# Gathers of half rows onto 128 partitions, with four 128x128 turns per tile, in a mixture-of-experts stage

## What is computed

```python
def hierarchical_moe(h, ...):          # h: 512 rows of 1024
    g_sel = argmax(softmax(h @ w_rg + b_rg))            # 1 of 4 groups
    e_logits = (h @ w_re + b_re)[group g_sel]           # 8 experts of it
    top_p, top_i = top_k(softmax(e_logits), 2)
    weights = top_p / sum(top_p) * p_gsel
    # for each row t and each of its 2 experts e, weight w:
    #   out[t] += w * (silu(h[t] @ w_gate[e]) * (h[t] @ w_up[e])) @ w_down[e]
```

## Time and profile before

| | us |
|---|---|
| Three runs, median (lowest to highest) | 1374.76 (1373.16 to 1378.31) |
| Profiled execution, its own time | 1375.67 |
| Its span, first to last instruction | 1374.0 |
| PE busy | 1277.7 (93%) |
| DVE busy | 611.6 (45%) |
| ACT busy | 351.0 (26%) |
| POOL busy | 158.7 (12%) |
| Mean granted TensorE clock | 0.976 of full speed |
| Read from HBM, written | 299.49 MB, 13.75 MB |

### The profile page before, as it was taken

The page is one execution under the profiler, slowest core; times in us unless marked ns, Lnnn a source line. Parts: engine busy times, 40 slices in busy tenths (PEclk is TensorE's granted clock), DMA queues, the critical chain, the costliest instruction groups (busy, mean ns, idle before and its releaser), DMA issues.

```text
span 1374.0 us, 20748 instructions
## 1 busy us (share of the span) xinstructions
PE 1277.7 (93%) x7392; PEld 637.2 (46%) x7393; DVE 611.6 (45%) x1058; ACT 351.0 (26%) x759; POOL 158.7 (12%) x278
## 2 busy tenths in 40 slices
PE   5999999999999999999999999989989987897887
PEld 1446656678844444644455545433333333332322
DVE  1667787874223343268787525212212212122225
ACT  1323233321144442212478310111101101010112
POOL 4011111111010000000000002311121121121110
PEclk9999999999999999999999999999999999899999
DMA  9163624331191110042131565879999999999995
GB/s 373 66 261 78 231 73 169 140 108 43 36 293 47 46 31 0 0 159 77 52 142 50 199 264 208 306 313 394 407 416 420 401 401 421 404 408 405 403 389 214
DMA packets 40570, 304.00 MB, mean 221 GB/s; under 512 B 7980, under 2 KB 8132, under 8 KB 22944
## 3 DMA queue, kind: packets, MB, share of 16 engines
q1 hardware_dynamic: 31952, 285.12, 52.9%
q0 software_dynamic: 8528, 17.67, 4.2%
HBM read 299.49 MB, written 13.75 MB: 228 GB/s over the span
## 4 chain that ended last, share of the span: by engine, by line
PE 72%; DMA 12%; DVE 9%; ACT 3%; issue 2%; POOL 1%; DVEq 0%; ACTq 0%; SPq 0%; POOLq 0%
PE bank L886 19%; PE bank L2994 13%; DMA arena<-in_w_down 9%; PE bank L3012 8%; PE bank L817 8%; PE bank L932 3%; PE bank L994 2%; PE bank L2979 2%; DMA arena<-in_ada_w 2%; DVE side L1524 1%; PE bank L1008 1%; PE bank L1238 1%; PE bank L1182 1%; PE bank L1159 1%; DVE X L3271 1%
## 5 line engine op out<-in xcount | busy, mean ns | idle before, releaser
L886 PE MATMUL bank<-hT,arena 128*128 128x512 f32 x656 | 290.0, 597 | 0.0
L2994 PE MATMUL bank<-arena,hT 128*64 128x512 f32 x1012 | 229.1, 603 | 16.6 <-DMA arena<-in_w_gu 15.2
L886 PEld LDWEIGHTS bank<-hT,arena 128*128 128x128 f32 x656 | 122.8, 191 | 147.0 <-issue 143.5
L2994 PEld LDWEIGHTS bank<-arena,hT 128*64 128x64 f32 x1012 | 71.8, 138 | 153.7 <-issue 134.6
L3012 PE MATMUL bank<-arena,yT 128*64 128x512 f32 x512 | 125.5, 635 | 12.7 <-DMA arena<-in_w_down 10.9
L3182 DVE TENSOR_SCALAR hT<-hT 128x256 f32<-128x256 f32 x32 | 9.4, 294 | 246.7 <-ACT hT L3120 246.7
L817 PE MATMUL bank<-arena,yT 128*128 128x512 f32 x256 | 114.8, 603 | 2.4 <-DVE yT L1785 2.3
L3120 ACT ACTIVATE hT<-bank 128x256 f32<-128x256 f32 x32 | 12.3, 383 | 263.2 <-PE bank L2994 263.2
L817 PEld LDWEIGHTS bank<-arena,yT 128*128 128x128 f32 x256 | 48.2, 192 | 60.3 <-issue 56.5
L3012 PEld LDWEIGHTS bank<-arena,yT 128*64 128x64 f32 x512 | 36.5, 145 | 76.9 <-issue 62.4
L932 PEld LDWEIGHTS bank<-arena 64*64 64x64 f32 x1856 | 59.4, 135 | 23.5 <-issue 13.1
(11 more groups left out here) (498 smaller groups left out, 1697.3 us busy)
## 6 DMA issues: line engine op xcount, KB each, us to landing
arena<-in_w_gu SPq DMA_DIRECT2D x62, 2048.0 KB, 24.5
arena<-in_w_down SPq DMA_DIRECT2D x32, 2048.0 KB, 30.6
arena<-in_w_in SPq DMA_DIRECT2D x53, 512.0 KB, 3.6
arena<-in_ada_w SPq DMA_DIRECT2D x24, 1024.0 KB, 5.2
arena<-in_w_ada SPq DMA_DIRECT2D x8, 1024.0 KB, 9.4
arena<-in_w_out SPq DMA_DIRECT2D x8, 1024.0 KB, 9.3
arena<-in_w_ada SPq DMA_DIRECT2D x8, 512.0 KB, 7.4
arena<-expert_rows SPq DMA_DIRECT2D x4, 1024.0 KB, 8.4
```

The source lines that it names most:

```text
L886: last = T.matmul(bank[0:rows, :], w[:, k, 0:rows], hT[:, k, :], start=k == 0, stop=k == KD - 1)
L2994: last = T.matmul(banks[1 + ub][MT * h:MT * h + MT, :], tile.xT[:, k, :], weights[:, :, 256 * h:256 * h + 256], start=k == 0, stop=k == KD ...
```

## The change

The rows are stored with permuted columns: column m*8 + k of a row goes to place k*128 + m. The DRAM scratch is seen as 1024 half rows of 2 KB. The numbers in `slots` are those of half rows, on all 128 partitions: positions 0 to 63 of a tile's first halves, then of its second halves. For that PE makes the slots' product twice, and DVE adds a column (`half_row`, -4 and -3) in the last of its three instructions. A gather brings 128 half rows onto 128 partitions x 512. Four transposes of 128 x 128 over contiguous columns take the place of eight of 64 x 128, and DVE's two instructions of `rows_in` read and write in another order. Two clears and the place of a one-row helper change with the buffers.

```diff
@@ -782,7 +782,11 @@
             V.wait_ge(s_sq_rows, NORM0 + TT * (i - 1) + t + 1)
             if i == 2 and t >= 2:
                 V.wait_ge(s_xnst, 16 * (t - 1))
-            dve.done(V.tensor_scalar(xn_tiles[i - 1][t], X[:, t, :], rstd[:, t:t + 1], None, MUL))
+            if i == 2:
+                dve.done(V.tensor_scalar(xn_tiles[1][t].rearrange("p (k m) -> p m k", k=KD),
+                                         X[:, t, :].rearrange("p (m k) -> p m k", k=KD), rstd[:, t:t + 1], None, MUL))
+            else:
+                dve.done(V.tensor_scalar(xn_tiles[i - 1][t], X[:, t, :], rstd[:, t:t + 1], None, MUL))
             V.sem_inc(s_xn, 1)
 
         def dve_hT_tile(i, t):
@@ -2311,7 +2315,8 @@
             pe_busy(bank, 7)
             eng.wait_ge(s_hot, 1)
             for n in range(2 * TT):
-                last = T.matmul(bank[0:MT, 0:NE + NOV], hot_pos[:, n, :], hot_tile[:, n, :], start=n == 0, stop=n == 2 * TT - 1)
+                for q in range(2):
+                    last = T.matmul(bank[MT * q:MT * q + MT, 0:NE + NOV], hot_pos[:, n, :], hot_tile[:, n, :], start=n == 0, stop=n == 2 * TT - 1)
             full(last)
             bank = fill(("places",))
             pe_busy(bank, 1)
@@ -2585,13 +2590,14 @@
         r_ones = ones[:, 0:NE]
         places = iotas[:, 0:NE + NOV]
         wts = sb("wts", [P, 2, TT])
-        slots = sb("slots", [MT, NE + NOV + 2], u32)
+        slots = sb("slots", [P, NE + NOV + 2], u32)
         ov_first = sb("ov_first", [1, 2 * NE - 2], i32)
         KEPT_AT = NE + 1
         last_hot = hT[:, 4, 0:TT * MT].rearrange("p (t m) -> p t m", m=MT)
         s_rt_in, s_rt_exp, s_routed = sem("router_ready_for_exp"), sem("router_exp_made"), sem("routed")
         s_xnst = sem("xn_stored")
         xn_dram = nc.dram_tensor("xn_scratch", [SEQ, DM], fp32, kind="Internal").ap()
+        xn_half = xn_dram.rearrange("t (h n) -> (t h) n", h=2)
 
         def bc(a, n):
             return a.rearrange("p (t o) -> p t o", o=1).to_broadcast([P, TT, n])
@@ -2676,10 +2682,9 @@
             dve.done(V.scalar_tensor_tensor(r_kept, r_nov[0:1, 0:NE - 3], 0.0, r_incl[0:1, 0:NE - 3], ALU.is_gt, MUL))
             V.tensor_copy(ov_first[:, KEPT_AT:KEPT_AT + NE - 3], r_kept)
             bank = take(V, ("slots",))
-            v = r_v[0:MT]
-            done(V.tensor_scalar(v, bank[0:MT, 0:NE + NOV], 0.0, 1024.0, ALU.is_equal, MUL))
-            empty(V, "dve", V.scalar_tensor_tensor(v, bank[0:MT, 0:NE + NOV], -1.0, v, ADD, ADD), ("slots",))
-            done(V.tensor_copy(slots[:, 0:NE + NOV], v))
+            done(V.tensor_scalar(r_v, bank[:, 0:NE + NOV], 0.0, 4.0 * SEQ, ALU.is_equal, MUL))
+            empty(V, "dve", V.scalar_tensor_tensor(r_v, bank[:, 0:NE + NOV], 2.0, r_v, MUL, ADD), ("slots",))
+            done(V.tensor_scalar(slots[:, 0:NE + NOV], r_v, half_row, 2.0, ADD, ADD))
             eng.sem_inc(s_routed, 1)
             second = hot_pos[:, TT:KT, :]
             done(V.tensor_scalar(r_half, second, 0.0, 0.5, ALU.is_gt, MUL))
@@ -2732,10 +2737,10 @@
 
         first, more_ = Steps("first"), Steps("extra")
 
-        tiles = [Tile(u, yflat[0:MT, 1024 * u:1024 * u + 1024], hflat[:, 512 * u:512 * u + 512],
+        tiles = [Tile(u, yflat[:, 512 * u:512 * u + 512], hflat[:, 512 * u:512 * u + 512],
                       hflat[:, 1536 + 256 * u:1792 + 256 * u], yflat[:, 3072 + 256 * u:3328 + 256 * u],
                       hflat[:, 2304 + 512 * u:2816 + 512 * u]) for u in range(U)]
-        extra = Tile("extra", side[0:MT, 0:1024], side[:, 1024:1536], side[:, 1536:1792], side[:, 1792:2048],
+        extra = Tile("extra", side[:, 0:512], side[:, 1024:1536], side[:, 1536:1792], side[:, 1792:2048],
                      cactB[:, :, :].rearrange("p k m -> p (k m)"))
         w_gu = [[sem(f"gate_up_loaded_{u}_{half}") for half in range(2)] for u in range(U)]
         w_dn = [sem(f"down_loaded_{u}") for u in range(U)]
@@ -2751,7 +2756,7 @@
         s_placed_col = [sem("first_places_picked"), sem("extra_places_picked")]
         s_extra_kept = sem("extra_rows_kept")
         place_col = sb("place_col", [P, U + 2], u32)
-        idx_col = sb("idx_col", [MT, U + 1], u32)
+        idx_col = sb("idx_col", [P, U + 1], u32)
 
         def stand_alone(eng):
 
@@ -2884,7 +2889,7 @@
             done = pool.done
             done(G.memset(ones_row, 1.0))
             eng.dma_start(gain_row, A["final_g"].rearrange("(o n) -> o n", o=1)).then_inc(s_gateB, 16)
-            done(G.memset(yflat[0:MT, 0:3072], 0.0))
+            done(G.memset(yflat[:, 0:512 * U], 0.0))
             done(G.memset(slots[:, NE + NOV:NE + NOV + 2], 4 * SEQ))
             eng.wait_ge(s_routed, 1)
 
@@ -2892,8 +2897,8 @@
                 G.tensor_copy(idx_col[:, i:i + 1], slots[:, bass.ds(e, 1)]).then_inc(picked, 1)
                 eng.wait_ge(picked, n + 1)
                 stand_alone(eng)
-                eng.indirect_dma_start(tile.xg, None, xn_dram, bass.IndirectOffsetOnAxis(ap=idx_col[:, i:i + 1], axis=0),
-                                       bounds_check=SEQ - 1, oob_is_err=False).then_inc(tile.gathered, 16)
+                eng.indirect_dma_start(tile.xg, None, xn_half, bass.IndirectOffsetOnAxis(ap=idx_col[:, i:i + 1], axis=0),
+                                       bounds_check=2 * SEQ - 1, oob_is_err=False).then_inc(tile.gathered, 16)
 
             def scatter(tile, steps, i, e, picked, n):
                 eng.wait_ge(steps.rows, n + 1)
@@ -2953,7 +2958,7 @@
             experts(eng, body)
 
         s_spread, s_copied = sem("last_places_then_gain_spread"), sem("last_places_then_gain_copied")
-        gain_row, ones_row = yflat[64:65, 0:DM], yflat[64:65, DM:DM + P]
+        gain_row, ones_row = yflat[64:65, 512 * U:512 * U + DM], yflat[64:65, 512 * U + DM:512 * U + DM + P]
 
         yg = slot_w[2][:, 0:8192].rearrange("p (n d) -> p n d", d=DM)
         finalG = slot_w[2][:, 8192:9216]
@@ -2975,8 +2980,8 @@
                     eng.wait_ge(steps.xT, n + 1)
                 eng.wait_ge(tile.gathered, (turn + 1) * 16)
                 stand_alone(eng)
-                for k in range(KD):
-                    last = T.transpose(banks[bank][:, MT * k:MT * k + MT], tile.xg[:, k::KD], ident[0:MT, 0:MT])
+                for j in range(KD // 2):
+                    last = T.transpose(banks[bank][:, CH(j)], tile.xg[:, CH(j)], ident[:, :])
                 last.then_inc(tile.xf, 1)
 
             def gate_up(tile, steps, u, e, n, ub, it=None, last_quarter=False):
@@ -3164,7 +3169,7 @@
             hidden_out(tiles[LAST[1]], first, NE - 1)
 
         def dve_experts(eng):
-            A2, B2 = (a.rearrange("p (k o) -> p k o", o=1).to_broadcast([P, KD, MT]) for a in (AB[2], modc[4]))
+            A2, B2 = (a.rearrange("p (q j o) -> p q j o", q=2, o=1).to_broadcast([P, 2, KD // 2, MT]) for a in (AB[2], modc[4]))
 
             for steps in (first, more_):
                 eng.sem_inc(steps.xT, 1)
@@ -3172,9 +3177,10 @@
             def rows_in(tile, steps, n, turn, bank=0):
 
                 eng.wait_ge(tile.xf, turn + 2)
-                V.tensor_tensor(tile.xT, b3(banks[bank][:, :], MT), A2, MUL).then_inc(steps.xT_own, 1)
+                xT = tile.xT.rearrange("p (q j) m -> p q j m", q=2)
+                V.tensor_tensor(xT, banks[bank][:, :].rearrange("p (j q m) -> p q j m", q=2, m=MT), A2, MUL).then_inc(steps.xT_own, 1)
                 eng.wait_ge(steps.xT_own, n + 1)
-                V.tensor_tensor(tile.xT, tile.xT, B2, ADD).then_inc(steps.xT, 1)
+                V.tensor_tensor(xT, xT, B2, ADD).then_inc(steps.xT, 1)
 
             def clamped(tile, steps, n):
 
```

## The result

The kernel after takes 1355.28 us (median of 6 runs, 1353.61 to 1357.33) against 1373.96 (median of 6) for the one before: a ratio of 0.9868, with a 95% interval of 0.985 to 0.9887. The medians lie 18.7 us apart, and by the ratio the kernel is 1.3% faster. The forecast was 1374.3, and the range of 1367 to 1380 doesn't hold the result. One of the runs of before took 1479.11 us: it was disturbed and is not in the ratio, but it is among the six of the median, which is 1373.16 without it (17.9 us).

The account below looks back on a forecast made before the run. The weights' DMA stream was taken to bound the experts' stage, so only PE's chain before 918 us counts: turns -1.9, slots' product +1.2, DVE +0.2, sum -0.5 us, forecast 1374.3, range 1367 to 1380.

Parts of the forecast that it names:

- a fixed amount of transfers: Behind SP's weight load issued at 918.04: the end is that issue plus these transfers plus a tail.
- Gathers on 128 partitions: Fetching the experts' rows: same bytes, order stays, 0 us for the transfers, bounds -0.3 and +0.6.
- The first, PE as the bound: Experts' stage: PE sets the end, so 28 turn groups behind 922 count, 13.4 us off, 1360.9; chance 0.03.
- The even engines: DMA engines' loads become even, so up to 6.2 us of idle time come back, 1368.1; chance 0.09.
- The late engines: DMA engines that end last get more gathered bytes, up to 9.9 us more, 1384.2; chance 0.07.
- Turns: Four groups on PE's chain before 918: each falls to 0.55 us, saving 0.48, together -1.9 us (1.1 to 2.3).
- The slots' product: PE before DVE's first slot instruction: 32 records instead of 16, +1.2 us, between 0.9 and 1.4.
- DVE's last slot instruction: DVE on the slots: a scalar from a column replaces a plain cast, 0.40 against 0.19 us, +0.2 (0 to 0.2).
- The permuted copy: DVE's four instructions of L785 keep 753 ns: 0 taken, 0 to +0.3 after 0.21 slack in a wait for PE.
- The clock: PE's granted clock on the chain: a dip lost or gained with the new timing is 2.6 us either way.

Follow-up runs that it names:

- turns_twice: The kernel after, with each of the four 128x128 turns of a tile made twice: 1356.66 us, ratio 0.9894.
- turns_in_a_row_before: The kernel before, with its eight turns taken over neighbouring columns instead of every eighth, so the result is another: 1370.74 us, ratio 0.999.

## Why the prediction was wrong

**The reading of the bound was right.** The stream ends the stage, PE's work behind 922 is hidden (turns_twice), and what counts is the start plus the bytes at the stream's rate. The share of 1.01 stayed, as forecast. What "a fixed amount of transfers" left out is that the rate is not fixed with the bytes.

**The step that failed** is "Gathers on 128 partitions", where I took 0 for the transfers, with bounds of -0.3 and +0.6 from "a few per cent of that half" of q0's 19.8 us. That counts a transfer by its own packets. On those I was off by 2.2 us, already outside the bounds. The large term is what it does to the packets of the other queue, 17.7 us, and no term of the sum stood for it. The rows at hand could have raised the question. The share was 1.01, but q0's 6.57 MB, some 4% of the bytes, went with a rate that stood below the 431 and 445 GB/s of two short stretches. From 1328 to 1331 the same engines, at a share of 1.02, moved 431; in the 408 us between, 407. Raising all of 922 to 1330 to even 425 is 17 us. A bound of the gain should have been taken from there: **a stream that is busy all the time and slower than elsewhere in the same trace has room in it**.

**The rivals.** None had this mechanism. The first, PE as the bound, gave 1360.9 and named as its sign that the end comes earlier while PE's waits for weights stay. That sign came and the rival is still wrong: the sign didn't tell it from a faster stream. The even engines aren't it: behind the last loads the share is 0.63 over 15 us where it was 0.59, so the engines still end far apart. The late engines got no more, as far as that share tells.

**The other terms.**
- Turns: 0.55 a group was forecast and 0.58 to 0.64 measured (0.44 at 881.86, with an issue of 0.13 behind it); right, though for another reason than the number of turns.
- The slots' product: +1.2 was forecast, and it cost 0. The 32 instructions take 1.16 us [after, 850.55], the 16 had taken 1.15. I had set the price by records, from a run of 32 at low clock, the places' product. That run takes 2.02 now in place of 2.85, at a granted clock of 1.00 in place of 0.62. It has as many instructions of the same form, but does first one half of the output partitions and then the other, where the slots' product alternates between them. By the two times the alternating pairs run beside each other; no run changed the order alone.
- DVE's last slot instruction: 0.26 us against 0.19, +0.07 where I had taken +0.2.
- The permuted copy: 0 was taken and 753 ns expected to stay. It takes 1342. On the chain that is 1.36 us at 833.65, 0.6 longer. From its start to the next instruction of DVE it is 0.54 more than before (833.65 to 835.15, and 832.91 to 833.87), beyond the bound of +0.3: the slack of 0.21 covers next to nothing. The Trainium skill (VectorE: DVE Perf Modes, What auto-detection actually checks) has the rule that I leaned on, even outermost counts; by it the 753 ns would have stayed, and this trace doesn't agree, 1342 ns.
- The clock: named as worth 2.6 us either way. The first gate and up product takes 7.09 us now and took 8.78 before, 1.7 less, and the places' product ahead of it 0.8 less. The stretch of that product, 852 to 855, was at a granted clock of 0.62 and is at 1.00; what tipped it was not tried by itself. In turns_in_a_row_before the product takes 1.89 us, ahead of the first turn and so of anything that this edit changes, and the rest follows: 7.09, and an issue at 914.40, in the one profile that there is. From 852 to 855 the granted clock is 1.00 in two of the four profiles with the slots' product of before and in all nine with that of after. The change may favour it, but it comes without the change too, so how much of these 2.5 us of the 2.9 is luck stays open. The rest comes out near even: the turns give some 1.7, the permuted copy takes 0.5, and PE's chain was 0.7 late (828.28 against 827.54) before it came to anything that the change touches.

**What stays open** is how the place acts. The runs show that only writes count, and only where 64 neighbouring partitions are their target. Those were 0 to 63 or 64 to 127 each time; no run tried 64 neighbours across the middle, so "neighbouring" and "in one half" aren't told apart. The Trainium skill (DMA: Bandwidth & Descriptors, Back-pressure in remote DMA) says of transfers between cores that a saturated SBUF port holds up the engines that write to it, and that stalled writes stall the engine's other queues as well. By that rule an engine's weights would wait behind its gathered rows, which has the direction of q1's 17.7 us; but these transfers stay on one core, and no run here shows a port.

## What to carry to other kernels

Where several queues share the DMA engines, price a small transfer by what the large stream loses while it is under way, and test that by letting it bring nothing (here 22 us for under 2% of the bytes). Beside such a stream, let indirect DMAs write to all 128 partitions, or to every other one, not to 64 that lie together. Compare the GB/s of a saturated stretch with the best stretch of the same trace before you call it full.

## What was not expected of the hardware

- The same weights' transfers run at 406 to 410 GB/s beside gathers onto partitions 0 to 63 (or 64 to 127) and at 422 to 425 beside gathers onto all, or onto every other partition. Scatters from 64 neighbouring partitions leave them at 423.
- 32 matmuls that alternate between the two halves of the output partitions take 1.16 us, as 16 onto one half (1.15); 32 that do one half after the other take 2.02.
- Eight 64x128 turns take 0.64 to 0.69 us when they read neighbouring columns and 1.02 to 1.08 when they read every eighth.
- DVE's multiplication of 128x1024 by a column: 753 ns in order, 1150 with a strided read, 1342 with a strided write.
